# Hybrid encoder block on one core: splits moved two blocks ahead, a row addition moved, the last norm taken apart

## The chip, the cores and the metric

One Trainium2 chip, one of its cores. The time is device microseconds from the start to the end of one execution; a kernel's time is the median of its runs.

## What is computed

One layer of a bidirectional encoder on 512 tokens of 1024 channels (16 learned tokens are put in front and dropped), all in float32: two token mixers, their gated merge, a post-norm, and then the part that this document is about, retrieval of experts (PEER).

```python
q = (x @ w_q)                                   # 8 heads, two halves of 128
s = einsum('blhpd,hpnd->blhpn', q, sub_keys)    # 128 keys per half
s_top, i_top = top_k(s, 16)                     # then the best 16 of the 256 pairs
expert = i1 * 128 + i2                          # 128 picks per token out of 16384
gate = softmax(best)
act = gelu(einsum('ld,lkd->lk', x, u_tab[e]))   # first layer
y = einsum('lk,lkd->ld', act * gate, v_tab[e])  # second layer, summed over heads
out = layer_norm(2**0.25 * x + y) * ln2_g + ln2_b
```

## The kernel before

A float32 matrix product is made of three bfloat16 products: each operand is split into a high half (a cast, on ScalarE) and a low half (value minus high half, on GpSimd or VectorE). `pair_matmul` (L146) issues the three products.

Of the 512 tokens 384 (three tiles of 128) go the dense way: for every block of 128 experts the first layer is formed for all tokens, times a grid of gates that is zero where an expert isn't picked. The last tile of 128 tokens goes the gathered way: for each of its 128 picks the expert's row of 1024 is fetched by an indirect DMA.

**First layer, dense (class Hidden, L1749 on).** 128 blocks. For block n SyncE loads `hid_u` (ring of 4), `split_hi` (L1791) casts it on ScalarE once block n-2 is formed (two slots), `split_lo` (L1809) subtracts on GpSimd, `form` (L1778) runs 24 matmuls on TensorE into one of two banks, `apply_gelu` (L1800) reads the bank on ScalarE, SyncE stores the result to DRAM. The 128 blocks run beside two other pieces of work.

**Retrieval (`retrieve`, L1900 on).** 72 blocks, in shares of 12, 20, 20 and 20, one share for each token tile. In each share TensorE makes the tile's scores, VectorE chooses the best keys and pairs, ScalarE takes an Exp before the last four blocks of the share, TensorE transposes the choice, ScalarE copies it out (L2017). From the second share on GpSimd gathers first-layer rows (L1866) behind low halves, and VectorE takes their dots (L1875). ScalarE's step is the high half of n+1, then the gelu of n.

**Scatter (`spread`, L2131 on).** 56 blocks. In the first 48 the grid of gates is made from the choice: for 16 tokens a turn, two blocks a turn, four groups u of four tokens. VectorE makes planes `place` and `second` (L2226) and their product with the weight (L2230) for each group, and behind the first three groups of a turn one dot (L1875). ScalarE makes the low halves of the product (L2269), TensorE multiplies (L2256), ScalarE evacuates the bank into the grid (L2280), whose first four spans of 64 tokens it also stores to DRAM, 512 KB each. GpSimd takes the first-layer low half of a block and behind it one gather (even blocks) or two (odd ones), into a ring of six rows. It begins with four gathers.

**Experts (`experts`, L2381 on).** 128 blocks. VectorE multiplies the stored first layer of the block by its part of the grid, from DRAM (L2479) and from the kept part (L2482), both in `ex_gated`; ScalarE casts it (L2455), VectorE takes the low half (L2484). ScalarE casts the second layer's block (L2452), GpSimd takes its low half (L2469). TensorE adds 18 matmuls of 128x512 into six banks that hold the whole sum for three tiles. For the gathered tile GpSimd fetches row n (L2464), ring of 4, and VectorE adds it times its gate to a running sum (L2489, L2493 for its start). Each engine's order is the order of the code:

```python
# ScalarE, block n          # GpSimd, block n         # VectorE, block n
v_hi(n)       # L2452       gather row n   # L2464    gating   # L2479, L2482
gated_hi(n)   # L2455       v_lo(n)        # L2469    gated_lo # L2484
                                                      add row  # L2489
```

ScalarE's `gated_hi` waits for the gating, and so the next block's `v_hi` stands behind it. SyncE loads block n+4 when `gated_lo` and `v_lo` of block n are done.

**Finish (`finish`, L2506 on).** Behind the experts VectorE adds the scaled input to the six banks (L2499), copies the gathered tile (L2502), and after a barrier takes the statistics of all four tiles (L2550), then ScalarE scales and shifts each tile (L2535), VectorE multiplies by the gain (L2563), GpSimd adds the bias (L2542), SyncE stores (L2526).

## Time and profile before

| what | us |
|---|---|
| median of 3 runs | 2753.62 |
| lowest, highest | 2751.52, 2768.15 |
| the profiled execution | 2751.31 |
| its span | 2749.5 |
| busy in it: PE, DVE, POOL, ACT | 2473.5, 1645.7, 1212.2, 1000.0 |

The first half of the span is the mixers, which the change does not touch. The retrieval's first-layer blocks begin at about 1528 us, the scatter stage at about 1860, the experts' at about 2182, and the last gating is at 2717 us.

### The profile page before, as it was taken

How to read it: one execution, taken by the hardware profiler on the slowest of the kernel's cores; microseconds unless marked ns; L12 is line 12 of the kernel's file. 1: busy time of each engine (PE TensorE's matmuls, PEld its weight loads, DVE VectorE, ACT ScalarE, POOL GpSimd, SP SyncE). 2: the span in 40 equal slices, each digit the busy share in tenths (PEclk: the TensorE clock that was granted, in tenths of full speed). 3: DMA queues.
4: the chain of work that ended last, by engine and by line, in shares of the span. 5: the costliest groups of instructions: out<-in, count | busy, mean ns of one | idle time of the engine just before them, and what ended most of it. 6: DMA issues, size and time to landing. Idle time of an engine off the chain costs nothing. (4 is left out here: it accounts for less than half of the span.)

```text
span 2749.5 us, 43135 instructions
## 1 busy us (share of the span) xinstructions
PE 2473.5 (90%) x14285; PEld 1391.9 (51%) x14285; DVE 1645.7 (60%) x3379; ACT 1000.0 (36%) x1741; POOL 1212.2 (44%) x744
## 2 busy tenths in 40 slices
PE   5999998986999999988979899997888899999995
PEld 3444443433777777776434455554555444444442
DVE  6123132015777777764250678898888477777777
ACT  4222212212333333332222334336888433333332
POOL 3312302312122222121504366675666677777775
PEclk9999999987999999999989999999999999999998
DMA  5301202220000000001314277787998899999995
GB/s 187 96 28 63 92 9 84 62 80 24 32 31 31 31 31 28 10 0 56 98 47 137 95 252 246 245 267 239 368 344 331 266 329 326 329 329 329 327 328 197
DMA packets 174308, 440.24 MB, mean 160 GB/s; under 512 B 17408, under 2 KB 83584, under 8 KB 174096
## 3 DMA queue, kind: packets, MB, share of 16 engines
q1 hardware_dynamic: 132752, 288.20, 30.6%
q0 software_dynamic: 36864, 134.23, 14.6%
q10 hardware_dynamic: 4608, 16.78, 1.6%
q8 instruction: 41, 0.67, 0.1%
q14 instruction: 43, 0.35, 0.0%
HBM read 395.11 MB, written 44.04 MB: 160 GB/s over the span
## 5 line engine op out<-in xcount | busy, mean ns | idle before, releaser
L149 PE MATMUL bank<-hT_hi,hid_u_hi 128*128 128x384 bf16 x1024 | 337.0, 329 | 67.3 <-POOL hid_u_lo L1813 40.0
L1813 POOL TENSOR_TENSOR hid_u_lo<-hid_u,hid_u_hi 128x1024 bf16<-128x1024 f32 x128 | 291.2, 2276 | 213.2 <-ACT hid_u_hi L1797 212.7
L149 PE MATMUL bank<-hT_lo,hid_u_hi 128*128 128x384 bf16 x1024 | 336.5, 329 | 0.0
L149 PE MATMUL bank<-hT_hi,hid_u_lo 128*128 128x384 bf16 x1024 | 336.2, 328 | 0.0
L204 POOL TENSOR_TENSOR ret_w_lo<-ret_w_raw,ret_w_hi 128x1024 bf16<-128x1024 f32 x72 | 152.7, 2154 | 394.0 <-ACT ret_w_hi L199 394.0
L2469 POOL TENSOR_TENSOR ex_v_lo<-ex_v,ex_v_hi 128x1024 bf16<-128x1024 f32 x128 | 272.2, 2127 | 120.9 <-ACT ex_v_hi L2452 120.9
L2435 PE MATMUL bank<-ex_v_hi,ex_gated_hi 128*128 128x512 bf16 x768 | 291.3, 379 | 27.8 <-DVE ex_gated_lo L2484 9.5
L2435 PE MATMUL bank<-ex_v_lo,ex_gated_hi 128*128 128x512 bf16 x768 | 291.6, 380 | 0.0
L2435 PE MATMUL bank<-ex_v_hi,ex_gated_lo 128*128 128x512 bf16 x768 | 291.6, 380 | 0.0
L2455 ACT ACTIVATE ex_gated_hi<-ex_gated 128x384 bf16<-128x384 f32 x128 | 66.9, 522 | 349.5 <-DVE ex_gated L2482 311.2
L2489 DVE SCALAR_TENSOR_TENSOR wide<-ex_row,row_gated,wide 128x1024 f32<-128x1024 f32 x128 | 164.7, 1287 | 41.9 <-DMA ex_row<-in_peer_v,row_index 40.9
L149 PEld LDWEIGHTS bank<-hT_hi,hid_u_hi 128*128 128x128 bf16 x1024 | 100.6, 98 | 154.2 <-issue 87.0
L2479 DVE TENSOR_TENSOR ex_gated<-ex_gated,ex_weights 128x256 f32<-128x256 f32 x128 | 171.4, 1339 | 0.0
L1316 POOL TENSOR_TENSOR dn_q_decayed<-dn_exp_b,dn_q_k 128x512 f32<-128x512 f32 x16 | 19.9, 1266 | 315.9 <-DVE dn_q_k L1405 315.9
L2435 PEld LDWEIGHTS bank<-ex_v_hi,ex_gated_hi 128*128 128x128 bf16 x768 | 74.8, 97 | 161.9 <-ACT ex_gated_hi L2455 43.5
L1805 ACT ACTIVATE hid_gelu<-bank 128x384 f32<-128x384 f32 x128 | 62.7, 490 | 257.4 <-PE bank L149 246.2
L2464 POOL DMA_INDIRECT ex_row<-in_peer_v,row_index x128 | 123.3, 963 | 28.6 <-DVE wide L2493 9.9
L149 PEld LDWEIGHTS bank<-hT_hi,hid_u_lo 128*128 128x128 bf16 x1024 | 100.9, 99 | 67.9 <-issue 2.5
L204 POOL TENSOR_TENSOR dn_w_lo<-dn_w_raw,dn_w_hi 128x1024 bf16<-128x1024 f32 x36 | 76.9, 2148 | 131.3 <-ACT dn_w_hi L199 131.3
L2452 ACT ACTIVATE ex_v_hi<-ex_v 128x1024 bf16<-128x1024 f32 x128 | 133.2, 1040 | 3.5 <-PEq L2181 3.5
L1797 ACT ACTIVATE hid_u_hi<-hid_u 128x1024 bf16<-128x1024 f32 x128 | 134.2, 1048 | 0.4 <-ACT ex_grid L2280 0.2
L149 PEld LDWEIGHTS bank<-hT_lo,hid_u_hi 128*128 128x128 bf16 x1024 | 100.7, 98 | 60.1 <-issue 2.0
(486 smaller groups left out, 5728.0 us busy)
## 6 DMA issues: line engine op xcount, KB each, us to landing
hid_u<-in_peer_u SPq DMA_DIRECT2D x128, 512.0 KB
ex_v<-in_peer_v SPq DMA_DIRECT2D x128, 512.0 KB, 5.4
ret_w_raw<-in_w_ret SPq DMA_DIRECT2D x60, 512.0 KB, 4.3
expert_hidden<-hid_gelu SPq DMA_DIRECT2D x128, 192.0 KB
ex_gated<-expert_hidden SPq DMA_DIRECT2D x128, 192.0 KB
dn_w_raw<-in_w_dn SPq DMA_DIRECT2D x36, 512.0 KB, 3.5
expert_weights<-ex_grid ACTq DMA_DIRECT2D x32, 512.0 KB
ex_weights<-expert_weights SPq DMA_DIRECT2D x64, 256.0 KB
```

The costliest lines, as they stand in the source:

```text
L149: last = nc.tensor.matmul(out, left[l], right[r], start=start and i == 0, stop=stop and i == len(PASSES) - 1)
L204: self.nc.gpsimd.tensor_tensor(self.pairs[slot][1][:, m % 4, :, :], self.raw[:, m % self.RING, :, :], self.pairs[slot][0][:, m % 4, :, :], ...
L1797: self.nc.scalar.activation(self.us[0][:, m % 2, :, :], self.u32[:, m % RING, :, :], ACT.Copy).then_inc(self.u_hi, 1)
L1805: self.nc.scalar.activation(self.act_out[:, m % RING, :], self.core.banks[4 + m % 2][:, 0:DENSE], ACT.Gelu).then_inc(self.gelu, 1)
L1813: self.nc.gpsimd.tensor_tensor(self.us[1][:, m % 2, :, :], self.u32[:, m % RING, :, :], self.us[0][:, m % 2, :, :], ALU.subtract).then_inc ...
L2435: last = nc.tensor.matmul(core.banks[u][:, :], gs[l][:, slot, t * P:(t + 1) * P], vs[r][:, slot, half * 512:(half + 1) * 512], start=first ...
L2452: nc.scalar.activation(vs[0][:, m % SLOTS, :], v32[:, m % RING, :], ACT.Copy)\
L2455: nc.scalar.activation(gs[0][:, m % SLOTS, :], g32[:, m % RING, :], ACT.Copy)\
L2464: nc.gpsimd.indirect_dma_start(row[:, n % RING, :], None, rows_dram[:, :], bass.IndirectOffsetOnAxis(ap=incoming.index[:, n:n + 1], axis=0))\
L2469: nc.gpsimd.tensor_tensor(vs[1][:, n % SLOTS, :], v32[:, n % RING, :], vs[0][:, n % SLOTS, :], ALU.subtract).then_inc(s["v_lo"], 1)
L2479: nc.vector.tensor_tensor(out_part, out_part, wt[:, m % RING // 2, :, m % 2, :], ALU.mult)
L2489: nc.vector.scalar_tensor_tensor(out=own[:, :], in0=row[:, m % RING, :], scalar=incoming.row_gated[:, cols], in1=own[:, :], op0=ALU.mult, ...
```

## The change

Four edits.

1. First-layer splits: two high halves before the first step, and each step is now the gelu of n, then the high half of n+2. GpSimd does the low halves of the scatter stage's first two blocks at the end of the retrieval, and in the scatter stage takes low half n+2 where it took n. In the first share of the retrieval ScalarE's Exp stands before the last block in place of the last four.
2. In the experts' step on VectorE the row addition (L2489) stands between the gating and the low half (L2484).
3. The scaled input of the three dense tiles enters the six banks by six float32 matmuls with 2^0.25 times the identity, before block 0, in place of six sums on VectorE at the end.
4. The last norm is done in the experts' stage, tile by tile, the gathered tile first: statistics straight from the banks, (x - mean) * gain, then times 1/std plus bias, all on VectorE, the square root on ScalarE, one store each. Gain and bias are loaded behind the last block's loads. `finish` and its barrier are gone.

```diff
@@ -1994,11 +1994,12 @@
                             g = 4 * (n + weights.blocks) + c
                             weights.hi(act, g, g, n % weights.blocks)
                 hidden.split_hi(act, 0, 0)
+                hidden.split_hi(act, 1, 1)
                 gathered.hold_x(act)
                 def step(n, m):
-                    hidden.split_hi(act, n + 1, m + 1)
                     hidden.apply_gelu(act, n, m)
+                    hidden.split_hi(act, n + 2, m + 2)
                 for t in range(NT):
                     for c in range(4):
@@ -2009,9 +2010,11 @@
                             score[:, 4 * c:4 * c + 4, :],
                             core.banks[c][:, :].rearrange("p (j n) -> p j n", j=4), ACT.Copy))
                     over_blocks(act, ends[t], ends[t + 1] - RING, step)
-                    act.wait_ge(exp_arg, t + 2)
-                    nc.scalar.activation(top[:, :, :], top[:, :, :], ACT.Exp).then_inc(exp_ready, 1)
-                    over_blocks(act, ends[t + 1] - RING, ends[t + 1], step)
+                    for n in range(ends[t + 1] - RING, ends[t + 1]):
+                        if n == ends[t + 1] - (RING if t else 1):
+                            act.wait_ge(exp_arg, t + 2)
+                            nc.scalar.activation(top[:, :, :], top[:, :, :], ACT.Exp).then_inc(exp_ready, 1)
+                        step(n, RING + n % RING)
                     bk.wait_full(act, "t", t)
                     j0 = 0 if t else 1
                     bk.reads("t", nc.scalar.activation(
@@ -2031,6 +2034,8 @@
                                 k < min((s - 1) * BESIDE_TILE + j + 1 + AHEAD, (NT - 1) * BESIDE_TILE):
                             gathered.gather(pool, k)
                             k += 1
+                for n in range(blocks, blocks + 2):
+                    hidden.split_lo(pool, n, n)
             @block.vector
             def _(dve):
@@ -2272,8 +2277,8 @@
                 def step(n, m, side, turn, in_span, u0):
-                    hidden.split_hi(act, n + 1, m + 1)
                     hidden.apply_gelu(act, n, m)
+                    hidden.split_hi(act, n + 2, m + 2)
                     for u in range(u0, u0 + per):
                         bk.wait_full(act, f"w{u}", turn)
                         token = in_span * TURN + u * G
@@ -2320,9 +2325,9 @@
                     span_steps(spans - 2 + side, side, False, side == 0)
                 def plain(n, m):
-                    if n < BLOCKS - 1:
-                        hidden.split_hi(act, n + 1, m + 1)
                     hidden.apply_gelu(act, n, m)
+                    if n < BLOCKS - 2:
+                        hidden.split_hi(act, n + 2, m + 2)
                 for n in range(blocks + busy, BLOCKS):
                     plain(n, RING + n % RING)
@@ -2334,7 +2339,8 @@
                     gathered.gather(pool, k, dots_before)
                 k = dots_before + RING
                 for n in range(blocks, BLOCKS):
-                    hidden.split_lo(pool, n, n)
+                    if n + 2 < BLOCKS:
+                        hidden.split_lo(pool, n + 2, n + 2)
                     for _ in range((1, 2)[n % 2] if n < blocks + busy else 1):
                         if k < PICKS:
                             gathered.gather(pool, k, dots_before)
@@ -2378,11 +2384,12 @@
-def experts(core, incoming, acc):
+def experts(core, incoming, a, acc, out, ident):
+    ORDER = (NT - 1,) + tuple(range(NT - 1))
@@ -2391,7 +2398,14 @@
-        names = "v_hi v_lo gated gated_hi gated_lo used row_added summed".split()
+        gain = sbuf(nc, ctx, "fin_gain", [P, D])
+        bias = sbuf(nc, ctx, "fin_bias", [P, D])
+        stats = sbuf(nc, ctx, "fin_stats", [P, NT, 12])
+        mv = sbuf(nc, ctx, "fin_mv", [P, NT, 2])
+        rstd = sbuf(nc, ctx, "fin_rstd", [P, NT])
+        scaled_ident = sbuf(nc, ctx, "ex_scaled_ident", [P, P])
+        names = ("v_hi v_lo gated gated_hi gated_lo used row_added summed ident_ready gb_in fin_steps var_ready std_ready "
+                 "row_ready stored").split()
@@ -2422,11 +2436,17 @@
+                sp.dma_start(gain[:, :], a["ln2_g"].partition_broadcast(P)).then_inc(s["gb_in"], 16)
+                sp.dma_start(bias[:, :], a["ln2_b"].partition_broadcast(P)).then_inc(s["gb_in"], 16)
+                for turn, tile in enumerate(ORDER):
+                    sp.wait_ge(s["row_ready"], turn + 1)
+                    sp.dma_start(out[tile * P:(tile + 1) * P, :], acc[:, tile, :]).then_inc(s["stored"], 16)
+                sp.wait_ge(s["stored"], 16 * NT)
-                    first, last_one = isinstance(n, int) and n == 0, isinstance(n, int) and n == BLOCKS - 1
+                    last_one = isinstance(n, int) and n == BLOCKS - 1
@@ -2434,12 +2454,16 @@
-                                                    start=first and i == 0, stop=last_one and i == 2)
+                                                    start=False, stop=last_one and i == 2)
+                pe.wait_ge(s["ident_ready"], 1)
+                for u, (half, t) in enumerate(UNITS):
+                    nc.tensor.matmul(core.banks[u][:, :], scaled_ident[:, :], acc[:, t, half * 512:(half + 1) * 512],
+                                     start=True, stop=False)
@@ -2456,6 +2480,10 @@
+                for turn in range(NT):
+                    act.wait_ge(s["var_ready"], turn + 1)
+                    nc.scalar.activation(rstd[:, turn:turn + 1], mv[:, turn, 1:2], ACT.Sqrt)\
+                        .then_inc(s["std_ready"], 1)
@@ -2480,87 +2508,58 @@
                     kept = grid[:, :, n, :] if isinstance(n, int) else \
                         grid[:, :, bass.ds(n, 1), :].rearrange("p s o t -> p s (o t)")
                     nc.vector.tensor_tensor(kept_part, kept_part, kept, ALU.mult).then_inc(s["gated"], 1)
-                    dve.wait_ge(s["gated_hi"], n + 1)
-                    nc.vector.tensor_tensor(gs[1][:, m % SLOTS, :], g32[:, m % RING, :], gs[0][:, m % SLOTS, :],
-                                            ALU.subtract).then_inc(s["gated_lo"], 1)
                     cols = slice(n, n + 1) if isinstance(n, int) else bass.ds(n, 1)
                     dve.wait_ge(row_in[m % RING], arrived(n, m))
                     dve.wait_ge(s["row_added"], n + RING)
                     nc.vector.scalar_tensor_tensor(out=own[:, :], in0=row[:, m % RING, :],
                                                    scalar=incoming.row_gated[:, cols], in1=own[:, :],
                                                    op0=ALU.mult, op1=ALU.add).then_inc(s["row_added"], 1)
+                    dve.wait_ge(s["gated_hi"], n + 1)
+                    nc.vector.tensor_tensor(gs[1][:, m % SLOTS, :], g32[:, m % RING, :], gs[0][:, m % SLOTS, :],
+                                            ALU.subtract).then_inc(s["gated_lo"], 1)
+
+                nc.vector.tensor_scalar(scaled_ident[:, :], ident[:, :], ALPHA, None, ALU.mult)\
+                    .then_inc(s["ident_ready"], 1)
                 nc.vector.tensor_scalar(own[:, :], acc[:, NT - 1, :], ALPHA, None, ALU.mult)\
                     .then_inc(s["row_added"], RING)
                 run(dve, step)
-                for u, (half, t) in enumerate(UNITS):
-                    dve.wait_ge(s["summed"], u + 1)
-                    part = acc[:, t, half * 512:(half + 1) * 512]
-                    nc.vector.scalar_tensor_tensor(out=part, in0=part, scalar=ALPHA, in1=core.banks[u][:, :],
-                                                   op0=ALU.mult, op1=ALU.add)
                 dve.wait_ge(s["row_added"], BLOCKS + RING)
-                nc.vector.tensor_copy(acc[:, NT - 1, :], own[:, :]).then_inc(s["row_added"], 1)
-                dve.wait_ge(s["row_added"], BLOCKS + RING + 1)
...
+                link = Chain(dve, s["fin_steps"])
+
+                def halves(tile):
+                    if tile == NT - 1:
+                        return [own[:, half * 512:(half + 1) * 512] for half in range(2)]
+                    return [core.banks[2 * tile + half][:, :] for half in range(2)]
+
+                def moments(turn, tile):
+                    for half, row_half in enumerate(halves(tile)):
+                        if turn:
+                            dve.wait_ge(s["summed"], 2 * tile + half + 1)
+                        ins = nc.vector.bn_stats(stats[:, turn, 6 * half:6 * half + 6], row_half)
+                    link(ins)
+                    link(nc.vector.bn_aggr(mv[:, turn, :], stats[:, turn, :]))
+                    nc.vector.tensor_scalar(mv[:, turn, 1:2], mv[:, turn, 1:2], LN_EPS, None, ALU.add)\
+                        .then_inc(s["var_ready"], 1)
+
+                def normalise(turn, tile):
+                    dve.wait_ge(s["std_ready"], turn + 1)
+                    link(nc.vector.reciprocal(rstd[:, turn:turn + 1], rstd[:, turn:turn + 1]))
+                    for half, row_half in enumerate(halves(tile)):
+                        cols = slice(half * 512, (half + 1) * 512)
+                        ins = nc.vector.scalar_tensor_tensor(out=acc[:, tile, cols], in0=row_half,
+                                                             scalar=mv[:, turn, 0:1], in1=gain[:, cols],
+                                                             op0=ALU.subtract, op1=ALU.mult)
+                    link(ins)
+                    nc.vector.scalar_tensor_tensor(out=acc[:, tile, :], in0=acc[:, tile, :],
+                                                   scalar=rstd[:, turn:turn + 1], in1=bias[:, :],
+                                                   op0=ALU.mult, op1=ALU.add).then_inc(s["row_ready"], 1)
+
+                dve.wait_ge(s["gb_in"], 32)
+                for turn, tile in enumerate(ORDER):
+                    moments(turn, tile)
+                    if turn:
+                        normalise(turn - 1, ORDER[turn - 1])
+                normalise(NT - 1, ORDER[NT - 1])
 def program(nc, a, out):
@@ -2606,8 +2605,7 @@
                     weights.open(queries, "top", 1, a["w_query"])
                     retrieve(core, weights, a, h1T, picked, hidden, gathered, incoming.grid, beside_retrieval, ident)
                 spread(core, a, picked, weights_dram, hidden, gathered, beside_retrieval, incoming)
-            experts(core, incoming, h0)
-        finish(core, a, h0, out)
+            experts(core, incoming, a, h0, out, ident)
 def shape_constants():
```

## Rows read from the trace of the kernel before

**Rows 1.** The page: its first line.

```profile
span 2749.5 us, 43135 instructions
```

**Rows 2.** Stretches: busy PE, PEld, DVE, ACT, POOL; clock, DMA, GB/s; last, L2256 alone.

```profile
1860.00:2144.00 284.00, 240.49 (x1920) 156.92 (x1920) 242.04 (x448) 230.49 (x576) 181.04 (x125) 0.98 0.88 321
2190.00:2700.00 510.00, 492.48 (x2196) 206.18 (x2195) 397.66 (x487) 178.48 (x243) 375.43 (x243) 1.00 0.96 328
...
1860.00:2144.00 284.00, 50.71 (x768) 46.92 (x768) 0.98 0.88 321
```

**Rows 3.** VectorE in time order, experts' stage, one block: start, duration, instruction.

```profile
2662.84 0.28 DVE L2482 TENSOR_TENSOR ex_gated<-ex_gated,ex_grid 128x128 f32<-128x128 f32 x1
2663.71 0.56 DVE L2484 TENSOR_TENSOR ex_gated_lo<-ex_gated,ex_gated_hi 128x384 bf16<-128x384 f32 x1 [0.59 <-ACT ex_gated_hi L2455]
2664.84 1.29 DVE L2489 SCALAR_TENSOR_TENSOR wide<-ex_row,row_gated,wide 128x1024 f32<-128x1024 f32 x1 [0.57 <-DMA ex_row<-in_peer_v,row_index]
2666.04 1.07 DVE L2479 TENSOR_TENSOR ex_gated<-ex_gated,ex_weights 128x256 f32<-128x256 f32 x1
```

**Rows 4.** ScalarE and GpSimd in the same block.

```profile
2663.16 0.52 ACT L2455 ACTIVATE ex_gated_hi<-ex_gated 128x384 bf16<-128x384 f32 x1 [2.73 <-DVE ex_gated L2482]
2663.59 1.04 ACT L2452 ACTIVATE ex_v_hi<-ex_v 128x1024 bf16<-128x1024 f32 x1
...
2658.59 0.96 POOL L2464 DMA_INDIRECT ex_row<-in_peer_v,row_index  x1
...
2664.70 2.13 POOL L2469 TENSOR_TENSOR ex_v_lo<-ex_v,ex_v_hi 128x1024 bf16<-128x1024 f32 x1 [0.96 <-ACT ex_v_hi L2452]
```

**Rows 5.** All 128 row additions: duration ns, shortest, median, longest.

```profile
L2489 DVE SCALAR_TENSOR_TENSOR wide<-ex_row,row_gated,wide x128: 1280/1289/1292, 2186.3 to 2718.7; 128x1024 f32<-128x1024 f32 x128
```

**Rows 6.** ScalarE, scatter stage: low halves, high half, and two gelus 40 blocks apart.

```profile
1962.64 2.44 ACT L2269 ACTIVATE spread_first_lo<-spread_place,spread_weight_low 128x128 bf16<-128x128 bf16 x8
1964.98 1.05 ACT L1797 ACTIVATE hid_u_hi<-hid_u 128x1024 bf16<-128x1024 f32 x1
...
1911.02 0.49 ACT L1805 ACTIVATE hid_gelu<-bank 128x384 f32<-128x384 f32 x1 [1.61 <-PE bank L149]
...
2137.37 0.49 ACT L1805 ACTIVATE hid_gelu<-bank 128x384 f32<-128x384 f32 x1 [1.31 <-PE bank L149]
```

**Rows 7.** The end: VectorE's sums and statistics, GpSimd's last addition, its store.

```profile
2718.21 0.56 DVE L2484 TENSOR_TENSOR ex_gated_lo<-ex_gated,ex_gated_hi 128x384 bf16<-128x384 f32 x1 [0.59 <-ACT ex_gated_hi L2455]
...
2719.88 3.76 DVE L2499 SCALAR_TENSOR_TENSOR h<-h,bank 128x512 f32<-128x512 f32 x6
2725.30 4.84 DVE L2550 BATCH_NORM_STATS2 fin_stats<-h 128x6 f32<-128x512 f32 x8 [0.53 <-PEq L2412]
...
2746.49 0.33 SPq L2526 DMA_DIRECT2D out<-h  x1
```

**Rows 8.** Waits of VectorE, experts' stage: us in total, times, longest.

```profile
DVE wide L2489 <- DMA ex_row<-in_peer_v,row_index: 40.1, 70, 1.3
```

**Rows 9.** The first low half of the stage, and GpSimd beside it.

```profile
2182.85 2.81 DVE L2484 TENSOR_TENSOR ex_gated_lo<-ex_gated,ex_gated_hi 128x384 bf16<-128x384 f32 x1 [0.59 <-ACT ex_gated_hi L2455]
...
2183.10 2.14 POOL L2469 TENSOR_TENSOR ex_v_lo<-ex_v,ex_v_hi 128x1024 bf16<-128x1024 f32 x1
```

**Rows 10.** A gather and the dot that waits for it, late and in the storing part.

```profile
2138.42 0.95 POOL L1866 DMA_INDIRECT ex_v<-in_peer_u_rows,row_index  x1
...
2143.60 1.22 DVE L1875 CUSTOM_DVE_ANT_0 ex_gated<-ex_v,wide 128x1024 f32<-128x1024 f32 x1 [2.60 <-DMA ex_v<-in_peer_u_rows,row_index]
...
1979.73 0.96 POOL L1866 DMA_INDIRECT ex_v<-in_peer_u_rows,row_index  x1
...
1988.92 1.22 DVE L1875 CUSTOM_DVE_ANT_0 ex_gated<-ex_v,wide 128x1024 f32<-128x1024 f32 x1 [2.09 <-DMA ex_v<-in_peer_u_rows,row_index]
```

**Rows 11.** TensorE's first block after tile 0's gathers, and the scatter stage's first.

```profile
1605.71 0.45 PE L149 MATMUL bank<-hT_hi,hid_u_hi 128*128 128x384 bf16 x1 [2.94 <-issue]
...
1868.84 0.50 PE L149 MATMUL bank<-hT_hi,hid_u_hi 128*128 128x384 bf16 x1 [10.27 <-POOL hid_u_lo L1813]
```

54 lines of the change are left out of this document (removed).

## The prediction

> **What bounds the kernel now.** I read the page first for the span [rows 1], then the table by stretches, then the timeline engine by engine, and last the waits.
>
> The experts' stage is the largest piece: 128 blocks, from 2182 us to 2719 us. TensorE is busy 492.48 of 510 us there and the DMA share is 0.96 [rows 2], so it looks bound by TensorE. It is not: its 18 matmuls take 492.48/122 = 4.04 us a block, and a block takes 4.19. The second gating (L2482) of one block ends at 2663.12, that of the next at 2667.31. Follow one block, with T = 2663.12, the end of the gating [rows 3, 4]. ScalarE starts the gated high half at T+0.04 and the next block's v high half at T+0.47, done at T+1.51. GpSimd starts the v low half at T+1.58 and holds it 2.13 us, to T+3.71. VectorE starts the next gating (L2479) at 2666.04 and finishes it at 2667.11: 0.28 us after GpSimd is done (2666.83), though it is a small instruction. It was held. L2482 then ends 0.20 us later (its 0.28 less an overlap of 0.08). 1.58 + 2.13 + 0.28 + 0.20 = 4.19: that loop, and no engine's total, sets the pace.
>
> The gated low half (L2484) is outside this loop today only because of where it stands: it runs from T+0.59 to T+1.15, before GpSimd begins. The row addition (L2489) stands behind it, beside GpSimd, and costs nothing: all 128 take 1280 to 1292 ns [rows 5].
>
> The scatter stage takes 5.66 us a block (1911.02 to 2137.37 over 40 blocks) [rows 6], and after the last gating there are 31.9 us to the end of the span [rows 1, 7].
>
> **The change part by part.**
>
> *Row addition before the low half: cost.* The question is when the row is there. Its gather is issued one block ahead, behind the v low half, at T-0.34; the row gathered at 2658.59 is added at 2664.84, so 6.25 us from issue to use [rows 3, 4]. 70 of some 121 additions wait for their row, 40.1 us in all [rows 8]; in the example the row comes at T+1.72. Those that do not wait start at about T+1.07, so the trace only says of them that the row was there by then. In the new order the addition begins when the row is there, X after T, and the low half 1.20 us later. With X above 0.38 that is past T+1.58, when GpSimd has begun. What a low half does then is in the trace once: the first of the stage began at 2182.85, GpSimd's v low half at 2183.10, and it took 2.81 us in place of 0.56, ending 0.42 us after GpSimd [rows 9]. So: low half done at T+3.71+0.42 = T+4.13, L2479 0.34 us more (0.42 unheld less the overlap), L2482 0.20, next T at T+4.67. That is 0.48 us a block. It is also the upper end, since X would have to pass 2.4 us to cost more, and none of the 70 waits is over 1.3 us.
>
> A longer block brings the row earlier in it, since two blocks pass between a gather's issue and its use: X = 3.85 + latency - 2 blocks. With 6.25 us and blocks of 4.19 this gives 1.72 as seen. With blocks of 4.67 and the same latency X is 0.76, held; with 5.6 us, a latency that I estimate for a stage with less traffic (5.18 us is that of a gather in the quiet part of the scatter stage [rows 10], 6.25 that of this one), X is 0.11, and a low half that starts before GpSimd delays it by little. Then the next block is short, its row late, and the one after is held again. I take two blocks in three held, 0.33 us a block: 126 blocks give 42 us. Nothing is gained where it is not held: ScalarE's order is as before, so GpSimd's start at T+1.58 is too, and VectorE still waits for it. Below zero is thereby excluded for this edit. The ends are 0 and 126 x 0.48 = 60 us; the held row is the instruction itself, so I stay near the upper end.
>
> The Trainium skill (SBUF — State Buffer, "SBUF: two separate sides") has it that VectorE and GpSimd share a port pair, held exclusively for a whole instruction, by VectorE also whenever it reads two SBUF inputs. For the tensor_tensor the trace agrees (2.81 for 0.56 us). For the row addition it does not: it reads two SBUF tensors and is never held [rows 5]. By the page, additions that start behind GpSimd would be held as well, and the one block in three with X above 1.58 would pay some 1.2 us more, 50 us in all; the measured rows decide, and I add nothing.
>
> *First-layer splits two blocks ahead.* In the plain course of blocks ScalarE's stream stays what it was (high half n+1, gelu n, high half n+2, ...); the split passes only what stands between two steps. In the scatter stage that is two evacuations, at some 0.5 us each as a gelu (0.49), and eight low halves, 2.34 us (1962.64 to 1964.98): 3.3 us [rows 6]. High half n+2 moves from behind them to right behind gelu n: it is ready 1.5 us after block n is formed instead of 4.8, and TensorE's stalls on first-layer low halves go. By that alone a block could shrink towards TensorE's work, 240.49/48 = 5.01 us, of which the scatter's matmuls are 50.71/48 = 1.06 [rows 2]. What is late next is on GpSimd's queue: the gathers stand behind low half n+2 now instead of low half n, so relative to TensorE they go out nearly two blocks later. The loop is: block n formed, gelu and high half 1.5, low half with its waits 2.3, so a gather 3.8 later; 5.2 to land (2138.42 to 2143.60); dot 1.2; the last group's place an estimated 0.4; its four low halves 1.2, half of the eight; its matmuls 0.5, half of 1.06: block n+2's matmuls end 12.3 us after n was formed. From there two forms and one scatter, 2 x 3.95 + 1.06 = 9.0, make block n+4 formed: four blocks take 21.3 us: 5.3 a block. Where the grid's stores are on the way a gather takes 9.2 us (1979.73 to 1988.92) [rows 10], which makes 25.3 and 6.3. With 5.66 before: 16 quiet blocks gain 0.35 each, 5.5 us; of 32 blocks in the storing spans I take those at the slow latency as a little over a third, so 5.3 x 0.63 + 6.3 x 0.37 = 5.67 for them, nothing. From below: all 32 at 6.3 cost 20 us; from above: 5.0 everywhere gains 32 us.
>
> *Scatter's first splits in the retrieval.* TensorE starts the scatter stage after 10.27 us of waiting for GpSimd, which had four gathers first [rows 11]. Now both splits are done in the retrieval. The retrieval's last high and low half lengthen it by 0.95 + 2.13 less the 0.48 of a copy: some 2.7 us. VectorE's first planes and dots still have to come, by gathers issued 2.7 us later, so only part of the wait goes. I count 3 us gained net, at least 0 and at most 8, of which 3 are given back because the stage's ramp is part of the quiet blocks above: together, scatter stage and its start, 5 us gained.
>
> *Retrieval.* TensorE's 2.94 us gap behind tile 0's four gathers [rows 11] goes, since low half 13 is out before them and 14 behind them. Tile 0's Exp moves behind three more blocks, which removes a ScalarE wait, but VectorE's choice of tile 0 sets when TensorE goes on, and three more low halves now fall beside its tensor_tensors: +1 us. At two tile ends a high half (0.95) stands before the copy that frees TensorE's bank: +2. Sum 0, between -3 and +3.
>
> *The last norm.* Today, after the last gating (2718.21 less the 0.59 us of waiting, T = 2717.62): six sums 3.76, a copy, a barrier, eight statistics 4.84, the norm in three engines, the last store at 2746.49, 3.0 before the end [rows 7]. New: addition and low half to T+2.8 (the row comes around T+1); VectorE then has four tiles of statistics, 2 x 0.61 + 0.45 each, and four normalisations, 0.2 + 2 x 0.63 + 1.25 + 0.1 each (0.68 and 1.28 are the nearest rows' durations): 4 x 4.5 = 18. Tile 3 fills the time in which TensorE forms the first sums. End at T+2.8+18+3.0 = T+23.9 against T+31.9: 8 us gained, 5 to 10. The six float32 identity matmuls run while TensorE waits for the first block, whose low half ends at 2185.66 [rows 9]; if they are late, TensorE catches up, its 4.04 us a block being under the loop's. The first block waits for its own row before its low half, which then falls beside the next v low half: 0.7 us once.
>
> **Sum.** 2751.3 (the profiled execution; span 2749.5) + 42 - 5 + 0 - 8 + 0.7 = 2781. The median of the runs shown is 2753.6, 2.3 above the profiled execution; I leave that difference out. 1% of this kernel, 27.5 us, is about what a measurement can tell from no change.
>
> **Rivals.**
> A. The low half is not held, or the row is there in time. Place: L2484. For it: 51 of 121 additions wait for nothing, and as the block lengthens rows come earlier; it decides from X below 0.1. Against: the 2.81 us row. Then 2781 - 42 = 2739, faster than before.
> B. Every low half is held: 60 in place of 42, 2799. For it: the latency of 6.25 us; against: traffic thins.
> C. The scatter stage does what its edit aims at: 5.0 us a block, 32 us in place of 5, with the cost in the experts' stage as forecast: 2754. Against: its dots already wait for rows, 2.09 and 2.60 us in two examples [rows 10].
>
> **Chances.** Forecast 0.50 (its own range 2766 to 2794), A 0.27, B 0.12, C 0.11. Low end 2738, where A lies; high end 2801, B. Faster by over 1% needs A and most of C together: 0.09. Slower by over 1% is above 2781: a little over half of the forecast's cases and all of B: 0.40. Within 1%: 0.51.
>
> **What would show it.** Right: VectorE's L2484 with a mean near 2 us and its end 0.42 us behind GpSimd's L2469; experts' blocks of 4.45 to 4.67 us; in the scatter stage more waits of the dots for rows, fewer of TensorE for low halves; a tail of some 24 us. Wrong: L2484 at 0.56 us beside GpSimd, or blocks at or under 4.19 us.

## The result, and the profile after

The changed kernel takes 2803.23 us (median of 4 runs, 2799.59 to 2803.99) where the kernel before takes 2752.57 beside it: a ratio of 1.0173, interval [1.0146, 1.0200]. The forecast was 2781 with a range from 2738 to 2801: the direction and the cause of the larger part are right, the scatter stage went against the forecast, the time came out 22 us above it and 2 us above the range, and slower by over 1% had a chance of 0.40 against 0.51 for within 1%. The profiled execution took 2803.27 us, of which the span is 2801.5, against 2749.5 before [rows 1].

Cut at five marks that both traces have (the gelus of blocks 71 and 119, the ends of the first and the last gating, the end of the span), the 52 us lie here:

| stretch, us | before | after | difference | forecast |
|---|---|---|---|---|
| start to gelu 71 (retrieval) | 1858.3 | 1860.3 | +2.0 | 0 |
| gelu 71 to gelu 119 (scatter stage) | 284.2 | 304.1 | +19.9 | -5, with the next row |
| gelu 119 to the first gating's end | 39.8 | 41.2 | +1.4 | |
| first to last gating's end (experts) | 535.4 | 569.0 | +33.6 | +42.7 |
| last gating to the end | 31.9 | 26.9 | -5.0 | -8 |

The table by stretches (TensorE, its weight loads, VectorE, ScalarE, GpSimd; clock, DMA share, GB/s) answers to [rows 2]. The first row is the scatter stage, the second 510 us of the experts' stage:

```profile
1860.00:2164.00 304.00, 251.41 (x1917) 160.93 (x1915) 234.28 (x443) 227.91 (x574) 175.04 (x122) 0.94 0.85 296
2215.00:2725.00 510.00, 454.52 (x2063) 197.43 (x2062) 434.13 (x457) 167.62 (x228) 373.96 (x229) 1.00 0.89 309
```

In 510 us of the experts' stage TensorE is busy 454.52 in place of 492.48 us, the DMA engines 0.89 in place of 0.96, while VectorE rises from 397.66 to 434.13. VectorE is busier while the stage goes slower, although its work is the same: some of its instructions must last longer. In this document an instruction is called held when it lasts longer than it does alone, because an instruction of another engine is in its way. The page's groups and the list of all executions of one line (shortest, median, longest, ns) name the instruction:

```profile
L2518 DVE TENSOR_TENSOR ex_gated_lo<-ex_gated,ex_gated_hi 128x384 bf16<-128x384 f32 x128 | 147.7, 1154 | 0.0
```

```profile
L2518 DVE TENSOR_TENSOR ex_gated_lo<-ex_gated,ex_gated_hi x128: 544/912/2505, 2210.9 to 2775.8; 128x384 bf16<-128x384 f32 x128
L2514 DVE SCALAR_TENSOR_TENSOR wide<-ex_row,row_gated,wide x128: 1274/1289/1291, 2209.7 to 2774.6; 128x1024 f32<-128x1024 f32 x128
```

The low half (L2518, before L2484, mean 0.58 us) now takes 1.15 us on average and up to 2.51; the row addition (L2514) is never held, as before [rows 5]. Both kinds of block stand next to each other in the timeline. VectorE:

```profile
2498.23 1.28 DVE L2514 SCALAR_TENSOR_TENSOR wide<-ex_row,row_gated,wide 128x1024 f32<-128x1024 f32 x1
2499.42 0.55 DVE L2518 TENSOR_TENSOR ex_gated_lo<-ex_gated,ex_gated_hi 128x384 bf16<-128x384 f32 x1
...
2506.82 0.28 DVE L2510 TENSOR_TENSOR ex_gated<-ex_gated,ex_grid 128x128 f32<-128x128 f32 x1
2508.26 1.29 DVE L2514 SCALAR_TENSOR_TENSOR wide<-ex_row,row_gated,wide 128x1024 f32<-128x1024 f32 x1 [1.17 <-DMA ex_row<-in_peer_v,row_index]
2509.46 1.75 DVE L2518 TENSOR_TENSOR ex_gated_lo<-ex_gated,ex_gated_hi 128x384 bf16<-128x384 f32 x1
2511.14 0.41 DVE L2507 TENSOR_TENSOR ex_gated<-ex_gated,ex_weights 128x256 f32<-128x256 f32 x1
2511.47 0.28 DVE L2510 TENSOR_TENSOR ex_gated<-ex_gated,ex_grid 128x128 f32<-128x128 f32 x1
```

and GpSimd beside it:

```profile
2499.89 2.40 POOL L2497 TENSOR_TENSOR ex_v_lo<-ex_v,ex_v_hi 128x1024 bf16<-128x1024 f32 x1 [0.96 <-ACT ex_v_hi L2476]
...
2508.68 2.13 POOL L2497 TENSOR_TENSOR ex_v_lo<-ex_v,ex_v_hi 128x1024 bf16<-128x1024 f32 x1 [1.29 <-ACT ex_v_hi L2476]
```

Where the row is there at once, the addition starts with the gating's end and the low half is out at 2499.97, as GpSimd begins. Where the row comes 1.17 us late, the low half starts at 2509.46 inside GpSimd's v low half (2508.68 to 2510.81) and ends at 2511.21, 0.40 us behind it; the next gating ends at 2511.75, 4.65 us after the one before (2507.10). Of the 126 blocks 66 take between 4.6 and 4.7 us and 55 between 4.1 and 4.5; 52% of all low halves are held. The mean is 4.459 us, where it was 4.194. Without the first block that is 126 x 0.264 = 33.3 us.

The waits of the scatter stage answer to [rows 10]:

```profile
DVE ex_weights L1875 <- DMA row_ring<-in_peer_u_rows,row_index: 28.4, 12, 5.4
DVE ex_gated L1875 <- DMA ex_v<-in_peer_u_rows,row_index: 28.0, 12, 4.9
PE bank L2261 <- DVE spread_second L2231: 36.8, 15, 5.1
```

The dots (L1875) wait for their rows up to 5.4 us at a time, and TensorE's scatter matmuls (L2261) wait just as long behind them. One such chain, across GpSimd, VectorE and ScalarE, in time order:

```profile
1981.48 0.96 POOL L1866 DMA_INDIRECT row_ring<-in_peer_u_rows,row_index  x1
...
1994.13 2.41 POOL L1813 TENSOR_TENSOR hid_u_lo<-hid_u,hid_u_hi 128x1024 bf16<-128x1024 f32 x1 [6.47 <-ACT hid_u_hi L1797]
1996.69 0.95 POOL L1866 DMA_INDIRECT ex_v<-in_peer_u_rows,row_index  x1
```

```profile
1989.84 1.22 DVE L1875 CUSTOM_DVE_ANT_0 ex_weights<-row_ring,wide 128x1024 f32<-128x1024 f32 x1 [3.01 <-DMA row_ring<-in_peer_u_rows,row_index]
```

```profile
1991.44 0.40 ACT L2274 ACTIVATE spread_first_lo<-spread_place,spread_weight_low 128x128 bf16<-128x128 bf16 x1 [5.06 <-DVE spread_place L2231]
...
1993.01 1.05 ACT L1797 ACTIVATE hid_u_hi<-hid_u 128x1024 bf16<-128x1024 f32 x1
```

A gather issued at 1981.48 is used at 1989.84, 8.4 us later; the dot lets VectorE go on, then ScalarE's low halves, the gelu and the high half of two blocks ahead, GpSimd's low half, and only behind that the next gathers, at 1996.69. The loop runs through the same engines as the forecast's, but by another way round. TensorE had been idle since 1988.0, so the block whose gelu stands at 1992.63 had been formed over 4 us before; the gelu and the high half behind it had waited on ScalarE, in order, behind the low halves of the planes (L2274, 5.06 us of waiting), and these for the dot.

The loss isn't spread evenly either. These are the distances between the gelus of blocks 80 to 112 in the changed kernel, one span of eight blocks a row; the third to the sixth of a row are long, but for one:

```text
5.7 4.8 9.7 6.4 7.0 6.5 5.2 5.1
5.9 5.1 9.8 6.6 7.8 6.3 5.2 5.2
6.5 4.8 10.1 6.1 7.1 5.1 5.7 5.1
5.8 5.1 9.5 6.7 7.1 6.5 5.2 5.2
```

ScalarE issues the eight stores of a span in its first half; in the third row they go out from 2028.9 to 2049.2 us and the long blocks run from 2034.9 to 2063.3. These sixteen blocks take 7.39 us on average, the sixteen others 5.34; before, both kinds took 5.65 to 5.67. So 16 x 1.73 = 28 us are lost and 16 x 0.33 = 5 gained.

The end, answering to [rows 7]:

```profile
2774.31 0.28 DVE L2510 TENSOR_TENSOR ex_gated<-ex_gated,ex_grid 128x128 f32<-128x128 f32 x1
...
2782.03 1.35 DVE L2538 BATCH_NORM_STATS2 fin_stats<-bank 128x6 f32<-128x512 f32 x2 [3.39 <-PE bank L2455]
...
2797.14 1.28 DVE L2553 SCALAR_TENSOR_TENSOR h<-h,fin_rstd,fin_bias 128x1024 f32<-128x1024 f32 x1
```

and TensorE's waits that answer to [rows 11]:

```profile
1592.59 0.69 PE L1980 MATMUL bank<-ident,top_chosen 128*128 128x128 f32 x2 [10.02 <-DVE top_chosen L2116]
...
1868.66 0.50 PE L149 MATMUL bank<-hT_hi,hid_u_hi 128*128 128x384 bf16 x1 [8.07 <-PEq L1932]
```

Tile 0's gap behind the gathers is gone, but TensorE now waits 10.02 us in one piece for VectorE's choice; the scatter stage starts after a wait of 8.07 us in place of 10.27.

### The profile page after: what moved, and what is told of

Its sections match the earlier page's. It is cut to its first block and busy times, and to the rows that moved or that the text cites. A ratio compares the mean times of both kernels' runs of the same rounds, so it can differ in the third digit from the quotient of the medians.

```text
span 2801.5 us, 43148 instructions
## 1 busy us (share of the span) xinstructions
PE 2482.8 (89%) x14297; PEld 1404.6 (50%) x14297; DVE 1701.7 (61%) x3385; ACT 994.2 (35%) x1740; POOL 1225.9 (44%) x740
## 5 line engine op out<-in xcount | busy, mean ns | idle before, releaser
L2455 PE MATMUL bank<-ex_v_hi,ex_gated_hi 128*128 128x512 bf16 x768 | 291.5, 380 | 64.2 <-issue 64.2
L2497 POOL TENSOR_TENSOR ex_v_lo<-ex_v,ex_v_hi 128x1024 bf16<-128x1024 f32 x128 | 286.7, 2240 | 134.1 <-ACT ex_v_hi L2476 134.1
L2455 PE MATMUL bank<-ex_v_hi,ex_gated_lo 128*128 128x512 bf16 x768 | 291.5, 380 | 0.0
L2455 PE MATMUL bank<-ex_v_lo,ex_gated_hi 128*128 128x512 bf16 x768 | 291.5, 380 | 0.0
L2514 DVE SCALAR_TENSOR_TENSOR wide<-ex_row,row_gated,wide 128x1024 f32<-128x1024 f32 x128 | 164.6, 1286 | 91.3 <-DMA ex_row<-in_peer_v,row_index 88.6
L2455 PEld LDWEIGHTS bank<-ex_v_hi,ex_gated_hi 128*128 128x128 bf16 x768 | 75.0, 98 | 178.8 <-issue 96.2
L1316 POOL TENSOR_TENSOR dn_q_decayed<-dn_exp_b,dn_q_k 128x512 f32<-128x512 f32 x16 | 19.9, 1268 | 315.8 <-DVE dn_q_k L1405 315.8
L2518 DVE TENSOR_TENSOR ex_gated_lo<-ex_gated,ex_gated_hi 128x384 bf16<-128x384 f32 x128 | 147.7, 1154 | 0.0
L2274 ACT ACTIVATE spread_first_lo<-spread_place,spread_weight_low 128x128 bf16<-128x128 bf16 x384 | 122.0, 394 | 66.1 <-DVE spread_place L2231 57.9
L2492 POOL DMA_INDIRECT ex_row<-in_peer_v,row_index x128 | 131.6, 1028 | 31.3 <-DVE wide L2523 12.5
```

The source lines that it names most:

```text
L2274: ins = nc.scalar.activation(first[1][:, u, i, :], place[:, u, i, :], ACT.Copy, scale=weight_low[:, tokens(u * G + i)])
L2455: last = nc.tensor.matmul(core.banks[u][:, :], gs[l][:, slot, t * P:(t + 1) * P], vs[r][:, slot, half * 512:(half + 1) * 512], start=False ...
L2492: nc.gpsimd.indirect_dma_start(row[:, n % RING, :], None, rows_dram[:, :], bass.IndirectOffsetOnAxis(ap=incoming.index[:, n:n + 1], axis=0))\
L2497: nc.gpsimd.tensor_tensor(vs[1][:, n % SLOTS, :], v32[:, n % RING, :], vs[0][:, n % SLOTS, :], ALU.subtract).then_inc(s["v_lo"], 1)
L2514: nc.vector.scalar_tensor_tensor(out=own[:, :], in0=row[:, m % RING, :], scalar=incoming.row_gated[:, cols], in1=own[:, :], op0=ALU.mult, ...
L2518: nc.vector.tensor_tensor(gs[1][:, m % SLOTS, :], g32[:, m % RING, :], gs[0][:, m % SLOTS, :], ALU.subtract).then_inc(s["gated_lo"], 1)
```

## The experiments

Twelve kernels, each timed beside the kernel before on the same chip. Line numbers in the rows are each kernel's own. (In x12's expectation, gating 71 to 119 means the gelus.) "Block" below is the mean distance between the ends of the second gatings (blocks 1 to 127), "scatter" the time from gelu 71 to gelu 119. Ratios are to the kernel before. The scatter stage is the same in before, x3, x7, x11 and x12 but for x12's swap, and the first four read 284, 282, 281 and 281 us: one trace against another differs by up to 3 us.

| kernel | us | ratio, interval | block | scatter |
|---|---|---|---|---|
| before (these runs) | 2748.7 | | 4.19 | 284 |
| after | 2803.2 | 1.0173 [1.0146, 1.0200] | 4.46 | 304 |
| x1 after, low half first | 2770.6 | 1.0080 [1.0063, 1.0097] | 4.22 | 305 |
| x2 after, gathers first | 2766.8 | 1.0066 [1.0049, 1.0083] | 4.46 | 273 |
| x3 before, row addition first | 2784.6 | 1.0130 [1.0113, 1.0147] | 4.45 | 282 |
| x4 after, other form of low half | 2802.2 | 1.0195 [1.0178, 1.0212] | 4.46 | 302 |
| x5 x1 and x2 | 2732.5 | 0.9937 [0.9923, 0.9951] | 4.22 | 269 |
| x6 x5, v high half ahead | 2730.7 | 0.9929 [0.9916, 0.9943] | 4.21 | 269 |
| x7 before, last norm alone | 2743.4 | 0.9976 [0.9966, 0.9985] | 4.22 | 281 |
| x8 before, splits alone | 2777.3 | 1.0096 [1.0080, 1.0111] | 4.20 | 308 |
| x9 x5, gating ahead | 2724.1 | 0.9905 [0.9889, 0.9920] | 4.13 | 272 |
| x10 x9, v high half ahead | 2698.9 | 0.9823 [0.9801, 0.9846] | 4.00 | 270 |
| x11 before, sum in SBUF | 2827.8 | single execution | 4.81 | 281 |
| x12 before, gathers first | 2751.5 | 1.0011 [1.0001, 1.0020] | 4.19 | 283 |

In x1, x5 and x7 nearly all blocks take 4.19 us as before; the 0.03 us in the mean are for the most part one block near the end (see x7).

### The experts' stage: which instruction is held

**x1: the changed kernel with the low half ahead of the row addition again.**

```diff
+dve.wait_ge(s["gated_hi"], n + 1)
+nc.vector.tensor_tensor(gs[1][:, m % SLOTS, :], g32[:, m % RING, :], gs[0][:, m % SLOTS, :], ALU.subtract)
 nc.vector.scalar_tensor_tensor(out=own[:, :], in0=row[:, m % RING, :],
...
-dve.wait_ge(s["gated_hi"], n + 1)
-nc.vector.tensor_tensor(gs[1][:, m % SLOTS, :], g32[:, m % RING, :], gs[0][:, m % SLOTS, :], ALU.subtract)
```

> The changed kernel with one edit undone: VectorE's low half of the gating stands before the row addition again. Theory (a low half behind the row addition falls beside GpSimd's v low half and is held until that ends): the experts' blocks go back from 4.46 to 4.19 us, 34 us less in that stage, 2803 - 34 = 2769; the scatter stage stays as it is in the changed kernel. Rival (the longer blocks come from the identity matmuls, the other loads or the later start of the stage, not from the order on VectorE): the blocks stay near 4.46 and the time near 2803.

33 us less than the changed kernel, one low half in 128 held, blocks of 4.19 again but for the one near the end. **x3** is the other way round, this one swap made in the kernel before:

> The kernel before with one edit alone: VectorE's row addition between the gating and its low half. Theory (held low halves): about half of the 128 low halves are held, blocks of 4.45 us in place of 4.19, 33 us more: 2786. Rival (the edit is free by itself and costs only together with the others): 2753.

36 us more than before, half of the low halves held. From the first to the last gating x1 takes 538.7 us, 30 less than the changed kernel, and x3 567.8, 32 more than the kernel before. So the order of two instructions is 30 to 32 of the 33.6 us of the table; the other 3 come with the last norm's edit (x7).

**x4: the same subtraction in another form**, to ask whether the tensor_tensor is what is held.

```diff
-nc.vector.tensor_tensor(gs[1][:, m % SLOTS, :], g32[:, m % RING, :], gs[0][:, m % SLOTS, :], ALU.subtract)
+nc.vector.scalar_tensor_tensor(out=gs[1][:, m % SLOTS, :], in0=g32[:, m % RING, :], scalar=1.0,
+                               in1=gs[0][:, m % SLOTS, :], op0=ALU.mult, op1=ALU.subtract)
```

> The changed kernel with the low half of the gating as a scalar_tensor_tensor, (gated x 1.0) - high half, in place of a tensor_tensor; its place behind the row addition stays. Theory (it is the form tensor_tensor that GpSimd holds up; the row additions, of the other form, are never held): no low half is held, each takes some 0.56 us beside GpSimd, blocks of 4.19 us or a little less, 34 us less: 2769. Rival (any VectorE instruction with these two inputs is held, and the row additions escape for another reason, as their inputs): low halves of up to 2 us remain and the time stays near 2803.

My theory fell. All executions of the line:

```profile
L2518 DVE SCALAR_TENSOR_TENSOR ex_gated_lo<-ex_gated,ex_gated_hi x128: 543/1125/2510, 2209.5 to 2774.3; 128x384 bf16<-128x384 f32 x128
```

A scalar_tensor_tensor is held as long as a tensor_tensor. So the form is not what frees the row addition. Its operands differ: the running sum `own` is `core.wide`, a PSUM tensor, so it has one SBUF input, and every held instruction has two.

**x11: the kernel before with that running sum in SBUF**, the direct test, executed once.

```diff
-        own = core.wide
+        own = sbuf(nc, ctx, "ex_own", [P, D])
```

> The kernel before, with the running sum of the row addition in an SBUF tensor in place of the PSUM tensor; everything else as it was. Theory (an instruction of VectorE is held beside GpSimd's low half of v when both of its inputs lie in SBUF, whatever the form; the row addition is free of it only since its running sum lies in PSUM): row additions are now held where they meet that low half, so their longest grows from 1.29 us to 2.5 us or more and their mean rises. Rival (the size or the operation frees it): all stay at 1.28 to 1.45 us, and the time within 6 us of before.

```profile
L2489 DVE SCALAR_TENSOR_TENSOR ex_own<-ex_row,row_gated,ex_own x128: 1276/1278/3422, 2184.6 to 2795.7; 128x1024 f32<-128x1024 f32 x128
```

The longest is 3.42 us, but all the others take 1.28: what I had expected happened to one addition in 128, and yet the kernel is 79 us slower (2827.8 to 2748.7). The timeline of a plain block shows why. VectorE, then GpSimd:

```profile
2401.30 1.28 DVE L2489 SCALAR_TENSOR_TENSOR ex_own<-ex_row,row_gated,ex_own 128x1024 f32<-128x1024 f32 x1
2402.49 2.35 DVE L2479 TENSOR_TENSOR ex_gated<-ex_gated,ex_weights 128x256 f32<-128x256 f32 x1
```

```profile
2401.81 2.75 POOL L2469 TENSOR_TENSOR ex_v_lo<-ex_v,ex_v_hi 128x1024 bf16<-128x1024 f32 x1 [0.96 <-ACT ex_v_hi L2452]
```

The addition began 0.51 us ahead of GpSimd, so this time GpSimd was the one held: its low half takes 2.75 us in place of 2.13 [rows 4], as 126 of the 128 do. 126 blocks x 0.62 = 78 us, the whole loss, and the block is 4.81 = 4.19 + 0.62. The 3.42 us addition is the first one, whose row came late. Either engine can be the one that waits. That is the rule of the Trainium skill (SBUF — State Buffer, "SBUF: two separate sides"): whichever starts first has the port pair for its whole instruction, VectorE's side counting when it reads two SBUF inputs while GpSimd's instruction reads SBUF. These runs agree with it in each direction, except on who is first, which the starts in the records don't tell (last section).

### The scatter stage: where the gathers stand

**x8: the kernel before with the splits' edit alone.**

> The kernel before with the first-layer splits two blocks ahead alone (retrieval and scatter stage as in the changed kernel). Theory (the scatter stage waits for its gathers, which stand behind the later low halves): 20 us more in the scatter stage and 2 in the retrieval: 2771. Rival (the splits cost only together with the other edits): 2749 or less.

28 us slower than before and scatter 308 us: this edit is the loss of the stage, by itself. The sign of the forecast's term for it was wrong.

**x2: the changed kernel with the gathers ahead of the low half on GpSimd.**

```diff
-                    if n + 2 < BLOCKS:
-                        hidden.split_lo(pool, n + 2, n + 2)
                     for _ in range((1, 2)[n % 2] if n < blocks + busy else 1):
...
                             k += 1
+                    if n + 2 < BLOCKS:
+                        hidden.split_lo(pool, n + 2, n + 2)
```

> The changed kernel with GpSimd's order in the scatter stage turned round: at each step the gathers stand before low half n+2, not behind it. Theory (the scatter stage lost 20 us because each gather goes out behind a low half that waits for a block formed later, so the dots and the planes behind them are late): gathers go out some 5 us earlier, the storing spans fall from 6.4 us a block to 5.7 or under, and 20 us or more come back: 2783 or less. Rival (the DMA queues are full in the storing spans, so that an earlier issue only waits longer): the dots still wait, spans stay over 6.2 us and the time over 2795.

36 us less, more than I expected: scatter is 273 us, 11 below the kernel before. **x12** asks whether the splits two ahead have any part in that, by the same swap in the kernel before:

> The kernel before, with its own order of the splits, but GpSimd issues the two gathers ahead of the low half in the scatter stage. Theory (the place of the gathers alone makes the storing stretches cheap, and the splits two blocks ahead are worth nothing by themselves): gating 71 to 119 falls from 284 us to 268 to 274, 2733 to 2739 us in all. Rival (the gain needs the splits two blocks ahead): 284 us as before, 2746 us or more; a result between would share it.

The rival is right. The swap alone gives 283 us, among the 281 to 284 of the unchanged stage. Waits between 1862 and 2130 us in the kernel before, then in x12 (us in total, times, longest):

```profile
PE bank L149 <- POOL hid_u_lo L1813: 25.9, 13, 10.3
DVE spread_place L2226 <- PE bank L2256: 13.4, 10, 3.6
DVE ex_gated L1875 <- DMA ex_v<-in_peer_u_rows,row_index: 8.9, 5, 2.2
```

```profile
DVE spread_place L2226 <- PE bank L2256: 41.2, 35, 1.9
PE bank L149 <- POOL hid_u_lo L1813: 26.0, 12, 11.5
```

The dots no longer wait for rows, but TensorE's waits for the first-layer low half stay (26.0 us), and VectorE now waits for TensorE instead (41.2 us for 13.4). Two waits stood side by side; each of the two edits removes one. Against the 281 to 284 us of the unchanged stage: splits alone (after, x1, x4, x8) +18 to +27 us, gathers alone nothing, both (x2, x5) -9 to -15.

**x5: both orders mended in the changed kernel.**

> The changed kernel with two pieces turned back or round at once: VectorE's low half before the row addition, and GpSimd's gathers before low half n+2 in the scatter stage. Theory (the two losses are in different stages and independent): the savings of the two runs alone, some 33 and 36 us, add up: 2803 - 69 = 2734, faster than the kernel before by 0.5%. Rival (one hides the other, for example because a scatter stage that ends sooner leaves the experts' stage with less loaded): over 2745.

2732.5 us, as expected, 17 us below the kernel before and 71 below the changed one. Blocks of the scatter stage, mean distance between gelus in each span of eight from block 72 on (spans 1 to 4, counted from 0, have the stores; the same four as the forecast's 32 blocks):

```text
before   5.98 5.66 5.66 5.65 5.69 5.64
after    5.68 6.28 6.47 6.32 6.38 5.54
x5       5.16 5.54 5.48 5.51 5.48 5.13
```

### The last norm

**x7: the kernel before with the identity matmuls and the last norm alone.**

> The kernel before with the identity matmuls and the last norm tile by tile alone. Theory (the end shrinks as in the changed kernel, from 31.9 to some 24 to 27 us after the last gating): 5 to 8 us less, 2741 to 2744. Rival (the identity matmuls or gain and bias loads cost at the start of the stage what the end gives): 2749.

6 us less, as expected, but it is made of two things. The time from the last gating to the end is 23.4 us in place of 31.9: 8.5 less, as forecast. And one block near the end takes 6.78 us in place of 4.19, since its row addition waits:

```profile
2712.09 1.29 DVE L2511 SCALAR_TENSOR_TENSOR wide<-ex_row,row_gated,wide 128x1024 f32<-128x1024 f32 x1 [3.81 <-DMA ex_row<-in_peer_v,row_index]
```

No such wait is over 1.5 us before it, or over 1.3 in the kernel before [rows 8]. That row's gather was issued at 2702.61, right behind SyncE's loads of gain and bias:

```profile
2702.01 0.46 SPq L2433 DMA_DIRECT2D fin_gain<-in_ln_g  x1
2702.52 0.55 SPq L2434 DMA_DIRECT2D fin_bias<-in_ln_b  x1
```

It took 9.5 us to land. Of the last four gathers one takes 7.0 to 10.4 us in every kernel with this edit whose trace shows the landings (x1, x2, x4 to x7, x9, x10), and none over 5.6 in those without (x3, x8, x11, x12); in x1, x2, x4, x5 and the changed kernel the row addition waits 2.4 to 4.7 us for it. So the rival is right in part: the two loads are the likely cause of some 3 us in the experts' stage. No run moved them alone.

### Further: the loop of the experts' stage

**x6: x5, with ScalarE making v's high half of n+1 ahead of its wait for the gating of n.**

```diff
+                value_hi(0, 0)
                 def step(n, m):
-                    value_hi(n, m)
+                    if not (isinstance(n, int) and n == BLOCKS - 1):
+                        value_hi(n + 1, m + 1)
                     act.wait_ge(s["gated"], n + 1)
```

Here `value_hi` is the cast of v with its waits.

> As x5_both_mended, and ScalarE makes the second layer's high half of block n+1 before it waits for the gating of block n. Theory (the pace of 4.19 us is the loop gating, ScalarE, GpSimd's v low half, held gating): with GpSimd's start cut loose from the gating the blocks fall to TensorE's 3.9 to 4.04 us, 126 x 0.15 to 0.3 = 19 to 37 us less: 2700 to 2715. Rival (VectorE's instructions then meet GpSimd's more often, or the DMA share of 0.96 is the next bound): blocks of 4.15 us or more, no gain on 2734.

The rival is right: 1.8 us less, nearly all blocks of 4.19. v's high half of one block still follows the gated high half of another on ScalarE, so the loop only changes its numbering; this I read from the code.

**x9: x5, with VectorE's step as low half n, gating n+1, row addition n.** `gate` is the two gating instructions.

```diff
+                gate(0, 0)
                 def step(n, m):
-                    gate(n, m)
                     dve.wait_ge(s["gated_hi"], n + 1)
...
+                    if not (isinstance(n, int) and n == BLOCKS - 1):
+                        gate(n + 1, m + 1)
                     dve.wait_ge(row_in[m % RING], arrived(n, m))
```

> The kernel with both things mended (2732.5) with VectorE's step in the experts' stage reordered: low half of block n, gating of block n+1, then the row addition of block n. Theory (the block of 4.19 us is a loop: the gating waits behind VectorE's low half and row addition, ScalarE's high half and GpSimd's low half of v wait for the gating): with the next gating ahead of the row addition both fall in the time in which GpSimd issues its gather, the loop is broken, and a block takes about what TensorE needs, 3.88 to 4.05 us: 126 x 0.15 to 0.30 = 19 to 37 us less, 2696 to 2714 us. Rival (the order only trades one held instruction for another, or the DMA engines, busy 0.89 of the stage, are next): the block stays at 4.15 or more, 2730 us or more.

Neither: 2724.1 us, 8 less than x5, between the two ranges, with blocks of 4.13. VectorE, then GpSimd, in one block:

```profile
2403.02 0.55 DVE L2514 TENSOR_TENSOR ex_gated_lo<-ex_gated,ex_gated_hi 128x384 bf16<-128x384 f32 x1
2403.49 0.41 DVE L2507 TENSOR_TENSOR ex_gated<-ex_gated,ex_weights 128x256 f32<-128x256 f32 x1
2403.82 2.21 DVE L2510 TENSOR_TENSOR ex_gated<-ex_gated,ex_grid 128x128 f32<-128x128 f32 x1
```

```profile
2403.49 2.39 POOL L2497 TENSOR_TENSOR ex_v_lo<-ex_v,ex_v_hi 128x1024 bf16<-128x1024 f32 x1 [0.63 <-ACT ex_v_hi L2476]
```

The first gating instruction gets through and the second is held in its place, since GpSimd's start hangs on the same gating by way of ScalarE. The loop is as it was, with one instruction less in it.

**x10: x9 and x6 together.**

> The kernel before this one, and ScalarE makes the high half of v of block n+1 ahead of its wait for the gating of block n. Theory: with VectorE's loop broken, ScalarE's order is the next link (v's high half behind the gated high half), so the block falls by a further 0.05 to 0.1 us, 6 to 12 us less than the kernel with the gating ahead. Rival: ScalarE is off the path, as it was with the old VectorE order, and the time is within 3 us of that kernel.

2698.9 us: 25 us less than x9, far more than the 6 to 12 expected, and 50 less than the kernel before. x6 alone gave nothing and x9 alone 8: as in the scatter stage, two links had to be cut together. Even so 56 of its 126 blocks still take 4.13 us; 51 take less than 4.05. Its stretch 2250 to 2630 us, and its waits in 2240 to 2640:

```profile
2250.00:2630.00 380.00, 374.33 (x1702) 162.94 (x1700) 369.85 (x379) 141.39 (x189) 309.34 (x190) 1.00 0.97 342
```

```profile
ACT ex_v_hi L2476 <- DMA ex_v<-in_peer_v: 103.4, 48, 4.4
```

TensorE is busy 374.33 of 380 us and the DMA engines 0.97; ScalarE now waits for the second layer's loads. Its 1702 matmuls are 94.6 blocks, so 3.96 us of TensorE a block for a block of 4.00: this stage is near what TensorE and the transfers allow. Of all kernels here this is the fastest.

## Why the prediction was right or wrong

**Experts, +42.7 forecast, +33.6 measured: mechanism right, size near.** The "low half done at T+4.13" after a late row is seen (0.40 us behind GpSimd, blocks of 4.65 for the 4.67 forecast). The step that was off is "two blocks in three held": it was 52%. Mostly two held blocks are followed by two that are not. After two held ones (9.3 us together) a row was always there at once, for x3 in all 30 such cases; after two short ones (8.5 us) it came 1.4 us late on average. The forecast's formula, with its 5.6 us, would have the second short block held too; the rows for these blocks landed 5.05 us after their issue (x3, mean of 31). "Nothing is gained where it is not held" was off too, by 0.06 us: with the first gating instruction before GpSimd's start, an unheld block takes 4.13. The first block cost 0.3 us (7.21 from first to second gating's end for 6.88), not 0.7. x1 and x3 confirm the cause from both sides, and put the order's share at 30 to 32 us; some 3 of the 33.6 belong to the last norm's edit.

**Scatter stage and its start, -5 forecast, +21 measured: this is the failed step.** It was priced as a loop through GpSimd's queue, 5.3 us a block at the quiet latency and 6.3 at the slow one, "a little over a third" of the 32 blocks at the slow one. The quiet price nearly holds (5.34 in the blocks of the storing spans away from the stores, 5.54 to 5.68 in the quiet spans). The slow one and its share do not: half of the 32 are slow, and at 7.39 us each. 32 x (6.36 - 5.67) = 22 us were lost, and 8 x (0.30 + 0.10) = 3 gained in the quiet spans, where 5.5 were forecast. What was wrong is the path: high half n+2 was to be "ready 1.5 us after block n is formed". That holds while nothing waits. ScalarE's gelu and high half still stand behind the low halves of the planes, and when a dot waits for its row these wait too. In the chain above the block was formed at 1988.0 and its high half done at 1994.06, 6 us later. So the loop gather, dot, low halves, high half, low half, gather closes over two blocks, 15.2 us (1981.48 to 1996.69), 7.6 a block, where the forecast had four blocks in 25.3. It isn't the latency: the eight rows that kept VectorE waiting for over 2.6 us in these spans were used 6.7 to 8.4 us after their issue, all below the 9.2 of the forecast. That the bound I gave ("all 32 at 6.3 cost 20 us") matches the outcome, and that the mean of the storing spans is 6.36, is chance: neither the 32 nor the 6.3 was there. The start's wait fell from 10.27 to 8.07 us only. The granted clock of the stage was 0.94 after and 0.98 before, 0.92 in x8, and 0.98 in x2. In the long stretches it was 0.88 to 0.94, after waits of TensorE such as 4.83 us up to 1992.85, and between them 1.00. TensorE was busy 21.2 to 22.9 us in each long stretch of four blocks and 19.8 to 20.1 in those between, so I estimate the clock's part at up to 10 us in all; no run separates it.

**Tail, -8 forecast, -5 measured; x7 -6 in all.** The size was right: from the last gating to the end x1, x2, x4, x5 and x7 take 23.4 to 23.7 us for the 23.9 forecast. The 26.9 of the changed kernel's profiled execution stand alone. In it too the 18 us of VectorE work were right: from 2782.03 to the last normalisation's end at 2798.4 it never waits for more than a record's gap. But VectorE waited 3.39 us for the bank (L2455) before the first dense tile's statistics, so "tile 3 fills the time" fell short by that: the row of the third block from the end had come 4.43 us late, the last two gatings came 2.20 us apart, and TensorE, after 2.67 us of idling and at a granted clock of 0.51 from 2772 to 2775 (the lower of its two levels), ended its last block 10.6 us behind the last gating (6.7 in x1 and x7). What the forecast put at nothing is the cost of the gain and bias loads, 2.4 to 3.5 us in one late block (x7, x5, x1), which the table counts with the experts' stage.

**Retrieval, 0 forecast, +2.0 measured**, inside its bounds of 3 each way. The gelu of block 71 stands at 1857.7 to 1861.1 us in the kernels with this edit and at 1857.6 to 1860.4 in those without, so the 2.0 us are no more than what traces differ by. VectorE's choice of tile 0 does set when TensorE goes on, as forecast.

**The rule weighed against the trace.** The prediction says of the row addition that "it reads two SBUF tensors and is never held", and sets the rows against the Trainium skill. The rows were right and my sentence wrong: one of the two inputs is in PSUM, so by the rule there is no hold, and there was no disagreement. It did no harm to the sum, which went by the rows. Rival A (not held) is refuted by the blocks of 4.65, C (5.0 a block) by the mean of 6.36, B (all held) by the 52%; C's mechanism is real only with the gathers moved (x5: 5.13 to 5.54). The total, 22 us above the forecast, is an experts' stage 9 us cheaper than forecast and a scatter stage, with its start, 26 us dearer, and 5 us of smaller ones.

## What to carry to other kernels

On an engine that runs its queue in order, ask of every instruction that waits for a transfer what stands behind it; here a 0.55 us subtraction behind a late row met GpSimd's long instruction and cost 0.46 us in every block in which it did. When work is moved ahead, move the DMA issues in front of it, not behind it: a gather that sits inside a loop adds its whole latency to every round. Follow such a loop through the order of every engine, and not only from the engine that you want to speed up: here ScalarE's order closed it over two blocks where I had counted four. And look at single blocks: a mean of 6.36 was made of 5.3 and 7.4. When a mended order moves nothing, look for a second wait that ends at nearly the same moment: twice here (gathers and splits, gating and v high half) neither edit alone gave more than 8 us, and the pairs gave 9 to 15 and 34.
